# Modulation row sums across partitions: 32 by 32 block transposes and group sums on VectorE, with four selector products on TensorE, in place of sixteen ones products

## What is computed

```python
silu_c = jax.nn.silu(c)
silu_cc = jax.nn.silu(c_ctx)
for l in range(DEPTH):                                  # DEPTH = 2
    m_lat = jnp.split((silu_c @ ada_w[l] + ada_b[l])[:, None, :], N_MOD, axis=-1)   # N_MOD = 9
    m_ctx = jnp.split(silu_cc @ ada_w[l] + ada_b[l], N_MOD, axis=-1)

    def half_ffn(t, m, j):
        h = modulate(rmsnorm(t, norm_g[l, j]), m[3 * j], m[3 * j + 1])
        return t + 0.5 * m[3 * j + 2] * swiglu(h, ffn_w_gate[l, j // 2], ffn_w_up[l, j // 2],
                                              ffn_w_down[l, j // 2])
    # x, ctx = half_ffn; Fourier (l = 0) or retention (l = 1) mixer; half_ffn
```

## Time and profile before

| | us |
|---|---|
| median of 3 runs | 3546.66 |
| lowest, highest | 3542.81, 3550.4 |
| the profiled execution, device time | 3541.26 |
| its span | 3539.5 |
| TensorE busy | 3431.8 (97%) |
| VectorE busy | 2032.4 (57%) |
| ScalarE busy | 1268.4 (36%) |
| GpSimd busy | 640.2 (18%) |

### The profile page before, as it was taken

How to read it: one execution, slowest core, us unless ns; L and a number is a source line. 1 busy time by engine, 2 the same in 40 slices (tenths; PEclk the granted TensorE clock), 3 DMA queues, 4 the chain that set the end, 5 groups by cost and what they waited for, 6 DMA issues and landing times.

```text
span 3539.5 us, 55525 instructions
## 1 busy us (share of the span) xinstructions
PE 3431.8 (97%) x22315; PEld 3109.0 (88%) x22315; DVE 2032.4 (57%) x2374; ACT 1268.4 (36%) x1678; POOL 640.2 (18%) x535
## 2 busy tenths in 40 slices
PE   7999999999999999999999999999999999998999
PEld 4888878888888888888999999989999999998999
DVE  3766836657766535545555456855545455864644
ACT  2222223212232124333434344355444444355443
POOL 2212303202221130002222220000323230000222
PEclk9999999999999999999999999999999999999999
DMA  5645504545355433334654654334565655343664
GB/s 195 189 149 155 161 22 123 173 140 175 107 172 167 130 97 89 90 95 140 184 173 140 182 166 138 108 114 131 158 183 165 184 167 155 108 120 93 177 184 143
DMA packets 862994, 507.89 MB, mean 143 GB/s; under 512 B 15060, under 2 KB 843024, under 8 KB 862800
## 3 DMA queue, kind: packets, MB, share of 16 engines
q1 hardware_dynamic: 862432, 503.74, 48.7%
q0 software_dynamic: 368, 1.38, 0.1%
HBM read 504.01 MB, written 1.05 MB: 143 GB/s over the span
## 4 chain that ended last, share of the span: by engine, by line
PE 87%; DVE 5%; ACT 4%; issue 2%; DMA 1%; POOL 0%; SPq 0%; DVEq 0%; POOLq 0%; ACTq 0%
PE bank L578 26%; PE bank L580 25%; PE bank L579 25%; ACT whi_all L1023 2%; PE bank L946 2%; PE bank L589 1%; DVE wlo_all L1271 1%; DVE t_full L1406 1%; PE bank L661 1%; PE bank L800 1%; PE bank L761 1%; PE bank L748 1%; PE bank L850 1%; PE bank L845 1%; DMA raw<-in_w_branch_a 1%
## 5 line engine op out<-in xcount | busy, mean ns | idle before, releaser
L1271 DVE TENSOR_TENSOR wlo_all<-raw,whi_all 128x1024 fp32r<-128x1024 f32 (+3 forms) x768 | 1015.1, 1323 | 972.1 <-ACT whi_all L1023 970.8
L578 PE MATMUL bank<-xn_hi,whi_all 128*128 128x256 f32 (+1 forms) x4608 | 1481.2, 321 | 18.6 <-DVE xn_lo L1395 11.4
L579 PE MATMUL bank<-xn_lo,whi_all 128*128 128x256 f32 (+1 forms) x4608 | 1447.4, 314 | 0.0
L580 PE MATMUL bank<-xn_hi,wlo_all 128*128 128x256 f32 (+1 forms) x4608 | 1447.2, 314 | 0.0
L1023 ACT CAST whi_all<-raw 128x1024 fp32r<-128x1024 f32 (+3 forms) x768 | 836.5, 1090 | 1032.6 <-PE bank L580 988.4
L578 PEld LDWEIGHTS bank<-xn_hi,whi_all 128*128 128x128 f32 x4608 | 882.6, 192 | 83.6 <-DVE xn_lo L1395 13.5
L580 PEld LDWEIGHTS bank<-xn_hi,wlo_all 128*128 128x128 f32 x4608 | 881.8, 191 | 52.3
L579 PEld LDWEIGHTS bank<-xn_lo,whi_all 128*128 128x128 f32 x4608 | 883.0, 192 | 49.5
L578 PE MATMUL bank<-h_hi,whi_all 128*128 128x256 f32 (+1 forms) x1408 | 459.0, 326 | 1.2 <-POOL h_lo L1767 1.2
L580 PE MATMUL bank<-h_hi,wlo_all 128*128 128x256 f32 (+1 forms) x1408 | 454.7, 323 | 0.0
L579 PE MATMUL bank<-h_lo,whi_all 128*128 128x256 f32 (+1 forms) x1408 | 454.4, 323 | 0.0
(11 more groups left out here) (247 smaller groups left out, 2802.2 us busy)
## 6 DMA issues: line engine op xcount, KB each, us to landing
raw<-in_ffn_w_in SPq DMA_DIRECT2D x176, 512.0 KB, 3.9
raw<-in_w_in SPq DMA_DIRECT2D x168, 512.0 KB, 3.8
ada_w<-in_ada_w SPq DMA_DIRECT2D x128, 512.0 KB, 4.0
raw<-in_ffn_w_gate SPq DMA_DIRECT2D x88, 512.0 KB, 3.8
raw<-in_ffn_w_up SPq DMA_DIRECT2D x88, 512.0 KB, 3.9
raw<-in_ffn_w_down SPq DMA_DIRECT2D x32, 768.0 KB, 5.2
raw<-in_ret_w_in SPq DMA_DIRECT2D x48, 512.0 KB, 3.8
raw<-in_ffn_w_out SPq DMA_DIRECT2D x32, 768.0 KB, 5.4
```

The source lines that it names most:

```text
L578: pe.matmul(o, whi[s][:, k, :], hi, start=(k == 0), stop=False)
L579: pe.matmul(o, whi[s][:, k, :], lo, start=False, stop=False)
L580: return pe.matmul(o, wlo[s][:, k, :], hi, start=False, stop=(k == ks - 1))
L1271: tt(wlo[s][:, 0:ks, :], raw[s][:, 0:ks, :], whi[s][:, 0:ks, :].bitcast(F32), ALU.subtract).then_inc(lo_done[s], 1)
```

## The change

After slot G + 1's ordinary work VectorE runs a new `group_row`. For each conditioning vector it transposes `ada_acc` in blocks of 32 by 32 (two instructions of 128 x 512, into the tiles `square` and `sumsq`, or, for the sixth row of a feed-forward, into two new tiles), and sums each block of 32 elements with two `tensor_reduce`. That leaves `ada_group`, 128 x 2 x 32: partition 32 q + c holds, for column block b, the sum of column 32 b + c over the 32 partitions of group q. TensorE's `ada_reduce(j)` is now one product of `group_sel` (a 128 x 128 selector that puts the sum of the four groups at partitions 32 j to 32 j + 31) with 16 columns of `ada_group`; the four products accumulate in the same 16 columns of bank 5. They stand ahead of the second to fifth group of three products in slot G + 2. The wait ahead of slot G + 2 is now for `ada_grouped`, which the last `tensor_reduce` raises, and for `sel_ready`. `group_sel` is made once at the start by a memset and one small `tensor_reduce`. `finish_row` is unchanged.

```diff
-            def ada_reduce(c, last):
-                for st in range(2):
-                    mm = pe.matmul(bank[5][:, 2 * c + st:2 * c + st + 1], ada_acc[st][:, c * P:(c + 1) * P], ones[:, 0:1],
-                                   start=True, stop=True)
-                if last:
+            def ada_reduce(j):
+                mm = pe.matmul(bank[5][:, 0:2 * DC].rearrange("p (k s) -> p k s", s=2),
+                               group_sel[:, 3 - j:7 - j, :].rearrange("p a b -> p (a b)"),
+                               ada_group[:].rearrange("p s (k j) -> p k s j", j=4)[:, :, :, j],
+                               start=(j == 0), stop=(j == 3))
+                if j == 3:
                     mm.then_inc(ada_cols, 1)
...
                         if row:
-                            pe.wait_ge(ada_sum, row[0] + 1)
-                            pe.wait_ge(ada_used[row[0] % 2], row[0] // 2 + 1)
+                            pe.wait_ge(sel_ready, 1)
+                            pe.wait_ge(ada_grouped, row_number[row[1:3]] + 1)
                         for k in range(ks):
...
-                            if row and k < DC:
-                                ada_reduce(k, k == DC - 1)
+                            if row and 1 <= k < 5:
+                                ada_reduce(k - 1)
...
+            def group_row(m):
+                l, j = ada_units[m][0:2]
+                late = any((l, j) in r and r.index((l, j)) == len(ROW_SLOT) - 1 for r in ADA_ROWS.values())
+                turned = ada_turned_dn if late else ada_turned
+                if not late:
+                    dve.wait_ge(ss_done, squares_summed[l, j])
+                dve.wait_ge(ada_sum, m + 1)
+                dve.wait_ge(ada_used[m % 2], m // 2 + 1)
+                for st in range(2):
+                    if st:
+                        link.after()
+                    for half in range(2):
+                        link(dve.transpose(turned[half][:], ada_acc[st][:, half * 512:(half + 1) * 512]))
+                    for half in range(2):
+                        link.after(link.n - 1 if half == 0 else None)
+                        i = dve.tensor_reduce(ada_group[:, st, 16 * half:16 * half + 16],
+                                              turned[half][:].rearrange("p (j c) -> p j c", c=32), AXX, ALU.add)
+                        if st == 0:
+                            link(i)
+                i.then_inc(ada_grouped, 1)
...
+                groups = {g: u for g, u in ada_slots(name, 1).items() if u[3] == DC - 1}
...
+                        if groups and SLOTS * r + s in groups:
+                            group_row(groups[SLOTS * r + s][0])
                         if units and SLOTS * r + s in units:
                             ada_unit(*units[SLOTS * r + s])
```

## The result

| | before | after |
|---|---|---|
| median of the runs, us | 3545.19 | 3654.80 |
| lowest, highest | 3542.81, 3550.4 | 3653.21, 3657.08 |
| span of the profiled execution | 3539.5 | 3651.4 |

The changed kernel takes 1.0308 times as long (95% interval 1.029 to 1.0325), 109.6 us more. 3671 was forecast, in a range of 3626 to 3718.

What follows compares the result with a forecast made beforehand. TensorE, busy for 97% of the span, was taken to bound the kernel. -64.1 + 17.3 + 141 + 30.4 = +124.6 us on 3541.3 gave 3665.9, with 5.4 for the median 3671; range 3626 to 3718.

Steps and rivals of the forecast that it cites:

- ones products and old waits removed: On TensorE, ones products cost 3.77 us a row, 60.3 in 16; with 3.8 us of waits, 64.1 us go.
- four new products: On TensorE in slot G + 2, eight records a row cost 1.08 us, 17.3 us in all.
- stall: TensorE idle ahead of slot G + 2 during evacuation, split and eight new VectorE instructions: 8.8 us a row, 141 us.
- clock: After each stall TensorE's clock is at 1.2 GHz for a while: 1.9 us a row, 30.4 us in all.
- The step that decides: At the head of slot G + 2, TensorE waits out VectorE's turn for slot G + 1: 8.8 us a row.
- two passes and 373 ns: Other prices of VectorE's transpose than 0.69 us: two passes, 3709 us, 14%; 373 ns without clock term, 3621, within a 17% rival.
- The sign to look for: In the changed profile, the granted clock is at 0.50 for some 4 us after each stall.
- Costed at nothing: The selector at the start, the wait for `ss_done`, and VectorE's new work of 83 us, already inside the stall.
- The one on the faster side: Rival: group sums are ready when TensorE comes, so only products count: 3500 us; 2%, and 1% within 0.2%.
- turning point: The change turns from gain to loss at a 2.9 us stall a row; evacuation and split alone take 2.97.
- The 3641 without the clock term: Rival's time if TensorE's clock holds through the stalls; 17%, together with the case of cheap transposes.
- VectorE falls behind: Rival: VectorE delays later splits; forecast to have no backlog, as TensorE stands still meanwhile; time the forecast's, no chance given.

Runs made afterwards that it cites:

- fill34: The changed kernel with 34 products of the identity by itself ahead of TensorE's wait, to keep TensorE busy through the stall; 3621.36 us, ratio 1.0231.
- dbl_group: The changed kernel with the eight transposes and reduces run twice, with the same result; 3745.63 us, 90.8 us above the changed kernel.
- early_late_mid: The changed kernel with transposes and reduces one turn earlier, and wait and four products ahead of the fifth to eighth group of slot G + 3; 3488.30 us, ratio 0.9856.
- early_late: The changed kernel with transposes and reduces one turn earlier on VectorE, and TensorE's wait and products one slot later, in slot G + 3; 3493.83 us, ratio 0.9872.
- wait_only: The kernel before, ones products kept, plus a TensorE wait for a VectorE `nop` behind the split of turn G + 1; 3632.57 us, ratio 1.0257.
- dbl_ones: The kernel before with each ones product issued twice, with the same result; 3624.77 us, ratio 1.0218.
- turn_plain: The changed kernel with a `nop` wait heading a plain slot G + 2, transposes behind the `nop`, four products in mid slot G + 3; 3520.15 us, ratio 0.9931.

## Why the prediction was right

| term | forecast | measured |
|---|---|---|
| ones products and old waits removed | -64.1 | -65.7 |
| four new products | +17.3 | +16.6 (1.04 a row, fill34) |
| stall | +141 | +129.8 |
| clock | +30.4 | +36 |
| sum | +124.6 | +117 |

- **What bounds it.** That only TensorE's queue counts held in every run: of VectorE's work that part was paid for which TensorE stood still, from all of it (`dbl_group`) to nothing (`early_late_mid`).
- **Removed.** 3.77 us a row was forecast, 3.75 measured in the mean. The 3.8 us of waits were short by 2, since the list of waits leaves out the smallest: the gaps at the 16 slots add up to 5.7.
- **The wait.** The step that decides was right in place and kind: 16 stalls, each released by the last `tensor_reduce`, the first part, up to the end of the split, 2.96 us a row where 2.97 had been read from the rows of before. Its size was 11 us too large. The chain of eight took 5.07 us and not 5.2: transposes of 0.66 to 0.71 us and reduces of 0.63 to 0.69, against 0.69 and 0.68. So both other prices fall, two passes and 373 ns. The figure of the Trainium skill (VectorE: DVE Perf Modes, The three transpose paths), from which I had estimated 1244 ns, doesn't carry over to 512 columns of four bytes: 0.70 us here. And I had added 0.5 us a row for GpSimd. Its pass does lie beside the first transpose (the row below), which at 132.68 took 0.70 us all the same. The lower bound, 0, was right; the row that I leaned on the earlier trace rows is one of an instruction with two operands from SBUF, and a transpose has one; whether that is the reason wasn't tested. That is 8 of the 11 us. Of the rest, 2 are the chain, and 1 is the overlap of the first transpose with the split.
- **The clock.** Right in kind, and 6 us too small: the row of before followed a wait of 4.84 us, in the first row here the clock was down until 4 us after the restart as there, and in the second, third and fifth kinds until 5.0 to 6.4 us after it. The sign to look for, some 4 us after each stall, was right for the other kinds (3.3 to 4.0).
- **Costed at nothing.** Held: in all 16 rows of the changed kernel the first transpose starts 0.08 us before the split's end, so nothing waited for `ss_done`; and `early_late_mid` has the selector, the wait for `ss_done` and all of VectorE's new work, and took 3488 us where 3492 had been worked out without any cost for them.
- **The number.** Its closeness is in part luck. The stall was 11 us too large and the clock 6 us too small, which offset each other. That 3671 lies 16 us above the measured 3655 is 8 us from the terms, 5 from the rest of the program, and 4 because I had put the median 5.4 us above the profiled execution, where it was 1.6.
- **The rivals.** The one on the faster side is real as a mechanism. It asked that the sums be ready when TensorE comes; in `early_late` they nearly are (2.8 us of waits are left), and the time is 3494, in `early_late_mid` they are, and it is 3488, where 3500 was written for it. The claim that the first part of the stall alone reaches the turning point couldn't be tested as meant, since the `nop` didn't wait for the split's end. The clock did not hold: it fell at all 16 stalls. The 3641 without the clock term was 3621 in `fill34`; the 20 us are mostly the 11 by which the stall was oversized and the 5 by which the median of before lay above its profiled execution. *VectorE falls behind* didn't happen, not even in `early_late_mid`, where nothing held TensorE back.

GpSimd's pass in the changed kernel, beside the first transpose (timeline of GpSimd):

```profile
131.84 2.04 POOL L1807 TENSOR_TENSOR h_lo<-silu_g,h_hi 128x512 f32 x1 [0.16 <-POOL h_hi L1805]
```

## What to carry to other kernels

Before work is moved from the bounding engine to an idle one, ask at which event the idle engine may begin and at which the bounding one asks for the result: here the eight instructions began at the event at which they were due, and made TensorE stand still for 130 us, so that the change lost 110; with the same instructions one turn earlier, and asked for a slot and a half later, it gains 53. A share of 57% doesn't say that work is hidden; the order of the two queues does. And a stall has a second price in TensorE's clock, here a quarter on top of its length.

## What was not expected of the hardware

- The clock, once brought down by a stall of only 1.5 to 1.9 us, stayed at 1.2 GHz for 14 to 17 us in 10 of 16 rows while products of one column stood between those of 512 (`wait_only`), and for 20 to 24 us with twice as many behind gaps of 0.6 to 1.1 us, in 3 of 5 rows (`dbl_ones`), although TensorE was busy all the time. After nearly the same stall with plain products it did not fall in any of 16 rows of the profiled execution (`turn_plain`). After stalls of 7.6 to 8.6 us it was down for 7 to 10 us in all, with eight short records in the slot behind.
- A VectorE `nop` behind a split raised its semaphore well before the split's end: TensorE, which waited for it, went on 1.0 to 1.8 us before that end in all 16 rows (`wait_only`).
- The block transpose and the `tensor_reduce` weren't lengthened beside GpSimd's pass (0.70 us for a transpose that lay wholly beside it, 0.64 to 0.65 for a reduce), where an instruction with two operands from SBUF took 2.32 instead of 1.28 us.
